# Three latent tiles projected for layer 1 inside layer 0's experts stage

## What is computed

```python
for l in range(2):
    last = l == 1
    h, hc = modulate(x, norm1_g[l], mod[0], mod[1]), modulate(xc, norm1_g[l], mod_c[0], mod_c[1])
    y, yc = token_mix(h, hc, ..., w_in[l], ..., not last)      # starts with h @ w_in: 1024 x 3104
    x = x + mod[2] * (y @ w_out[l])
    h2 = modulate(x, norm2_g[l], mod[3], mod[4])
    x = x + mod[5] * peer_ffn(h2, peer_wq[l], peer_subkeys[l], peer_u[l], peer_v[l])
    # layer 0 does the last three lines for the context xc too
return rms_norm(x, final_g)

def modulate(x, g, shift, scale): return rms_norm(x, g) * (1 + scale) + shift
def peer_ffn(h, ...):              # per token: 8 heads choose 16 experts each, 128 in all
    act = gelu(einsum('td,thkd->thk', h, u[eid]))             # u[eid]: one row of 4 KB per expert
    return einsum('thk,thkd->td', gate * act, v[eid])
```

## Time and profile before

| | us |
|---|---|
| median of 3 runs (lowest, highest) | 5386.06 (5382.54, 5390.33) |
| the profiled execution | 5427.65 |
| its span, first to last instruction | 5425.9 |
| granted TensorE clock over the span, mean | 0.705 |
| layer 0's last step (gelu start to gelu start) | 2581 to 2950 |
| the V rows that remain after it | 2950 to 3163 |
| layer 1's projection stage | 3168 to 3424 |

### The profile page before, as it was taken

How to read it: one execution, slowest core, us unless ns; L and a number is a source line. 1 busy time by engine, 2 the same in 40 slices (tenths; PEclk the granted TensorE clock), 3 DMA queues, 4 the chain that set the end, 5 groups by cost and what they waited for, 6 DMA issues and landing times. The chain is left out here.

```text
span 5425.9 us, 35743 instructions
## 1 busy us (share of the span) xinstructions
PE 2597.9 (48%) x11633; PEld 1150.5 (21%) x11633; DVE 2785.2 (51%) x6161; ACT 494.5 (9%) x1038; POOL 2963.2 (55%) x2672
## 2 busy tenths in 40 slices
PE   5977778323333333333333569668601233333344
PEld 2435555200010000000000134355400000000001
DVE  1138658976466465565443011664897646644410
ACT  1027520000000000000000000443000000000000
POOL 1003103877777777777776620130287777777765
PEclk9988998656656656566666789789755565655567
DMA  5401024899999999999999941012389999999998
GB/s 189 149 24 18 2 92 161 298 375 379 369 369 375 375 372 376 372 369 368 374 380 362 365 151 62 8 19 84 104 296 361 365 363 361 360 361 365 366 364 321
DMA packets 452198, 1468.20 MB, mean 271 GB/s; under 512 B 59259, under 2 KB 97359, under 8 KB 448943
## 3 DMA queue, kind: packets, MB, share of 16 engines
q0 software_dynamic: 368640, 1342.34, 65.8%
q1 hardware_dynamic: 72360, 99.62, 5.7%
q10 hardware_dynamic: 11014, 23.95, 1.4%
HBM read 1459.62 MB, written 6.13 MB: 270 GB/s over the span
## 5 line engine op out<-in xcount | busy, mean ns | idle before, releaser
L1812 DVE CUSTOM_DVE_ANT_0 experts_U<-experts_U,Y 128x1024 f32<-128x1024 f32 x1280 | 1566.8, 1224 | 1353.4 <-DMA experts_U<-in_peer_u_dram,experts_expert 1270.2
L1458 POOL DMA_INDIRECT experts_U<-in_peer_u_dram,experts_expert x1280 | 1383.3, 1081 | 1005.2 <-DVE experts_expert L1315 611.4
L1697 PE MATMUL experts_acc<-experts_V,experts_lent 128*32 128x512 f32 x4544 | 983.4, 1002 | 1836.0 <-DMA experts_V<-in_peer_v_dram,experts_turned 1774.7
L1473 POOL DMA_INDIRECT experts_V<-in_peer_v_dram,experts_turned x1136 | 1274.6, 1122 | 505.5 <-issue 336.0
L1697 PEld LDWEIGHTS experts_acc<-experts_V,experts_lent 128*32 128x32 f32 x4544 | 191.4, 153 | 2558.2 <-issue 2557.5
L371 PE MATMUL proj_acc<-proj_w,HT 128*128 128x512 f32 (+2 forms) x1280 | 486.4, 540 | 2.9 <-DVE PR L426 2.9
L734 POOL MEMSET glascore_Q<- 128x4096 f32 x2 | 7.0, 3512 | 560.4 <-POOLq L101 560.4
L371 PEld LDWEIGHTS proj_acc<-proj_w,HT 128*128 128x128 f32 x1280 | 242.0, 191 | 244.6 <-issue 213.6
L426 DVE COPY PR<-proj_acc 128x512 f32<-128x512 f32 (+2 forms) x80 | 49.5, 622 | 404.6 <-PE proj_acc L371 404.6
L1793 DVE TENSOR_TENSOR experts_lent<-experts_acc,experts_G 128x1024 f32<-128x1024 f32 x10 | 12.2, 1222 | 414.4 <-PE experts_acc L1697 351.1
L1226 PE MATMUL experts_keys<-experts_sub,experts_QT 64*128 64x128 f32 x320 | 41.5, 398 | 337.5 <-DVE experts_rest L1244 236.4
(11 more groups left out here) (259 smaller groups left out, 3165.3 us busy)
## 6 DMA issues: line engine op xcount, KB each, us to landing
experts_YT<-in_ada_w_dram SPq DMA_DIRECT2D x24, 1024.0 KB
proj_w<-in_w_in_dram SPq DMA_DIRECT2D x10, 2048.0 KB, 7.9
experts_U<-in_peer_u_dram,experts_expert POOLq DMA_INDIRECT x1280
experts_V<-in_peer_v_dram,experts_turned POOLq DMA_INDIRECT x1136
proj_ada<-in_ada_w_dram ACTq DMA_DIRECT2D x16, 1024.0 KB, 4.9
setup_ada<-in_ada_w_dram SPq DMA_DIRECT2D x8, 1024.0 KB, 17.5
experts_U<-in_w_out_dram SPq DMA_DIRECT2D x4, 2048.0 KB, 11.3
experts_V<-in_peer_wq_dram SPq DMA_DIRECT2D x4, 2048.0 KB, 21.4
```

What stands on the lines that cost most here:

```text
L1458: pool.indirect_dma_start(s.U[:, n % RING], None, u_rows, bass.IndirectOffsetOnAxis(ap=s.expert[:, j % 2, k:k + 1], axis=0)).then_inc(ug[n ...
L1473: pool.indirect_dma_start(into, None, v_rows, bass.IndirectOffsetOnAxis(ap=s.turned[:, i % 2, e:e + 1], axis=0)).then_inc(done, 16)
L1697: mm = nc.tensor.matmul(acc[32 * c:32 * c + 32, i % 2, half], s.spread[:, e * 32:e * 32 + 32], v_slot(V * GROUP + c)[0][:, 512 * half:512 ...
L1812: nc.vector.tensor_tensor_reduce(out=s.U[:, n % RING], in0=s.U[:, n % RING], in1=s.H[:, tiles[j]], scale=1.0, scalar=0.0, op0=ALU.mult, op ...
```

## The change

The constant `HIDDEN` = 3 is added: three latent tiles (3, 4, 5) of layer 1's projection are made in layer 0's experts stage.

- `experts` takes its tiles in the order 3, 4, 5, 2, 0, 1 in layer 0 (3, 4, 5, 2 in layer 1), so that the three are finished in `X` when the last step begins. `QT` is indexed by place in that order.
- In layer 0's last step SP broadcasts the three rows of layer 1's first norm, ACT squares the three tiles (into `half_out`) and loads w_in of layer 1 in 13 chunks of 240 columns (the last of 224) into two buffers in `QT`, VectorE scales and shifts, TensorE transposes through the search's PSUM banks `ps`, ACT copies into `Y`. From group 12 of the step on, TensorE does two products of 240 columns behind each group of V: 39 in all. ACT copies each out and stores it to the DRAM tensor `kept`.
- `project` in layer 1 norms and projects tiles 0, 1 and 2 only (17 products in place of 38), with the same seven chunks of weights. ACT loads the three kept tiles from DRAM into `PR` behind its part of the norm and waits for them before the stage ends.

The core of the diff, with the helper functions cut (their bodies are told above):

```diff
+HIDDEN = 3
 def project(nc, m, l, HT, PR, scratch):
+    t1 = NT - HIDDEN if last else NT
+    EARLY = min(t1 - 1, BANKS)
-        work = [(c, t) for c, (_, _, need) in enumerate(PROJ_CHUNKS) for t in range(NT) if need or not last or t >= CT]
+        work = [(c, t) for c in range(len(chunks)) for t in range(t1) if chunks[c][2] or not last or t >= CT]
             def _(act):
                 if not first:
+                    for t in range(t1, NT):
+                        act.dma_start(PR[:, t], m.pr[(t - t1) * P:(t - t1 + 1) * P]).then_inc(kept, 16)
+                    act.wait_ge(kept, 16 * HIDDEN)
                     return
 def experts(nc, m, l, t0, Y):
-    tiles = list(range(t0, NT))
+    tiles = list(range(NT - HIDDEN, NT)) + list(range(CT, NT - HIDDEN)) + list(range(t0, CT))
+        WIDTHS = [240] * 12 + [PROJ - 12 * 240]
+        units = [(c, i) for c in range(len(WIDTHS)) for i in range(HIDDEN)]
+        UNITS_AT = [(T - 1) * GROUPS + g for g in range(12, 32) for _ in range(2)][:len(units)]
+        TURN_AT = [(T - 1) * GROUPS + g for g in (8, 9, 11)]
+        MEAN_AT, SHIFT_AT, COEF_AT = [24, 30, 36], [27, 33, 39], 6
+                def load_chunk(c):
+                    act.dma_start(next_w[:, c % 2, :, 0:WIDTHS[c]], ...).then_inc(next_win[c % 2], 16)
+                def next_unit(u):
+                    c, i = units[u]
+                    act.wait_ge(next_prods, u + 1)
+                    if u >= 4:
+                        act.wait_ge(next_stored[u % 4], 16 * (u // 4))
...
+                    nc.scalar.activation(next_out[:, u % 4, 0:WIDTHS[c]], ps[:, u % 2, 0:WIDTHS[c]], ACT.Copy).then_inc(next_ev, 1)
+                    act.wait_ge(next_ev, u + 1)
+                    act.dma_start(m.pr[i * P:(i + 1) * P, 240 * c:240 * c + WIDTHS[c]], ...).then_inc(next_stored[u % 4], 16)
+                    if u == last_unit[c] and c + 2 < len(WIDTHS):
+                        load_chunk(c + 2)
+                def next_product(u):
+                    c, i = units[u]
+                    if i == 0:
+                        pe.wait_ge(next_win[c % 2], 16 * (c // 2 + 1))
+                    if u >= 2:
+                        pe.wait_ge(next_ev, u - 1)
+                    for k in range(KD):
+                        mm = nc.tensor.matmul(ps[:, u % 2, 0:WIDTHS[c]], next_HT[:, k, i * P:(i + 1) * P],
+                                              next_w[:, c % 2, k, 0:WIDTHS[c]], start=k == 0, stop=k == KD - 1)
+                    mm.then_inc(next_prods, 1)
```

More of the change, by code:

```diff
@@ L257, in norm_modulate @@
     ev0, ev1 = ht
-    tiles = list(range(t0, NT))
+    tiles = list(range(t0, t1))
     n = len(tiles)
-    streams = [0, 1] if t0 < CT else [1]
+    streams = [x for x in (0, 1) if any((t >= CT) == x for t in tiles)]
     @block.sync
@@ L377, in early @@
                     product(pe, i - 1)
-            norm_modulate(nc, m, l, m.a["norm1_g"][l], 0, 0, HT, st, block, ht, scratch, after=early, squares=not first)
+            norm_modulate(nc, m, l, m.a["norm1_g"][l], 0, 0, t1, HT, st, block, ht, scratch, after=early, squares=not first)
             @block.sync
             def _(sp):
-                for c, (c0, wd, _) in enumerate(PROJ_CHUNKS):
+                for c, (c0, wd, _) in enumerate(chunks):
                     if c >= WR:
@@ L1700, in _ @@
                         mm.then_inc(sums, 1)
+                    if more:
+                        for i in range(HIDDEN):
+                            if TURN_AT[i] == G:
+                                next_turn(i)
+                        for u in range(len(units)):
+                            if UNITS_AT[u] == G:
+                                next_product(u)
             @block.vector
```

120 lines of the change are left out of this document (106 added, 14 removed).

## The result

| kernel | runs | median us | range us |
|---|---|---|---|
| before | 4 | 5384.3 | 5381.8 to 5390.33 |
| changed | 4 | 5311.3 | 5305.31 to 5316.15 |

The ratio is 0.9862, 95% interval 0.9845 to 0.9879: the kernel is 73 us faster. The forecast was 5299.4 us, 87 us faster, in a range of 5270 to 5345. The direction and the range hold; the gain is 14 us less than forecast.

What follows compares the result with a forecast made beforehand. Layer 0's experts stage was taken as bound by its gathers (DMA), layer 1's projection by TensorE. Terms -121.5 + 32 + 1.3 + 1.5 = -86.7 us, from 5386.1 to 5299.4 us, range 5270 to 5345.

Steps and rivals of the forecast that it cites:

- The projection stage, -121.5 us: Layer 1's projection: 124.9 us of products and 3.1 of transposes leave TensorE, 6.5 us of waits for weights come.
- rival 4: Layer 1's projection: the kept tiles' 4.77 MB run into the weight loads and delay a chunk; 5317 us, chance 0.07.
- The clock and TensorE: Layer 0's last experts step: at clock 0.9 a group takes 9.3 of 11.5 us, products stay beside gathers; 0 us.
- Rival 2: Layer 0's last step: clock stays low and TensorE ends the groups, 102 us; 5369 us in all, chance 0.08.
- Weight chunks in time: Layer 0's last step: each chunk is needed 23 us after its load goes out; one landed in 12 us.
- rival 3: Layer 0's last step: weight loads starve behind gathers, TensorE waits, gathers run out of slots; 5454 us, chance 0.06.
- Rings and tables: Experts stage: ring stalls 0 (10 us in the range), gelu table reload 1.28 us, semaphores 1.5 us for both stages.
- The bytes, +32 us: Layer 0's last step: 19.05 MB added beside the gathers, priced between a lower end of 6 us and 51.
- the middle between 14 and 51: Price of the added bytes: 14 us at a 410 GB/s ceiling, 51 us at the full 374 GB/s byte price.
- Rival 1: Layer 0's last step: added bytes are absorbed like the adaLN loads, 6 us in place of 32; 5273 us, chance 0.12.
- the rule of the Trainium skill's page: DMAs issued from SP, ACT and GpSimd share the same 16 engines, so another queue brings no bandwidth: 51 us.

Runs made afterwards that it cites:

- few_matmuls: Changed kernel with one matmul in place of eight in each of the 39 moved products: 5095.0 us, against 5097.5 for the changed kernel.
- more_bytes: Changed kernel with nine more loads of 1 MB on SP's queue in the last step: 5134.7 us, against 5106.4 for the changed kernel.
- first set: Follow-up runs, on chip 12, of four partial versions of the change beside the kernel before, which took 5432.9 us there.
- third set: Follow-up runs on chip 0: kernel before 5158.6 us, changed kernel 5106.4, and two variants of the changed kernel with fewer or more bytes loaded.
- second and third set: Follow-up runs on chips 7 and 0: kernel before 5159.7 and 5158.6 us, unaltered changed kernel 5097.5 and 5106.4 us, beside variants of it.
- part2_alone: Changed kernel doing all moved work in layer 0's experts stage while layer 1's projection still makes all six tiles: 5470.5 us, against 5432.9 for the kernel before.

## Why the prediction came out as it did

- **The projection stage, -121.5 us:** right, and near in its terms. 121.5 us in the traces, 122.8 in the runs; TensorE's busy time in the stage falls by 125.8 us (238.0 to 112.2) for 128.0 forecast, the waits for weights are 4.74 and 0.99 us for 4.5 and 1.0. That the sum agrees to the tenth is luck. The kept tiles' 4.77 MB delayed nothing, so rival 4 falls.
- **The clock and TensorE:** right. 0.91 in the stretch of the products for the 0.9 taken, and in `few_matmuls` seven eighths of the moved products are worth 0 us in the step, 2.5 by the medians and 5 by the ratios. Rival 2 falls.
- **Weight chunks in time:** right. 2.3 us of waiting for them in the whole step; rival 3 falls for this kernel, though `more_bytes` shows that its chain exists.
- **Rings and tables:** the gelu's table 1.28 us as taken; the end of layer 0's experts stage 0.9 to 1.6 us for at most 1.4 (layer 1's was not read). VectorE's waits had more weight than I gave them: 14.3 us in place of some 10, with 3 us of gathers lost for 0.
- **The bytes, +32 us:** this is the term that was mis-sized, and the step that failed stands behind the sum: the profiled execution was 0.8% over the median, no stage looked disturbed, and so the difference was taken as it is. Some 25 us of the 0.8% lay in steps that the change doesn't touch, and the price of the bytes was another where these ran faster. The term was near right where I read it (31 us in the traces, 37.7 in the runs of the first set) and too small for the median runs of the result (48) and for faster ones (55 by the traces of the third set, 59 to 69 by the medians). The 32 itself was a choice, the middle between 14 and 51, so that it came within 1 us of the traces is luck. Its upper end was no bound either: the 51 us price a byte at 374 GB/s, while the added rows got 342 GB/s of engine time, 56 us for 19.05 MB. The mechanism, bytes that fill the slack first and are paid in full beyond it, fits both sets, but in the third the gathers got dearer too; that the slack was there in the runs was assumed.
- **Rival 1** (absorbed like the adaLN loads) falls everywhere: the step grew by 35 us and more. By the rule of the Trainium skill's page "DMA: Bandwidth & Descriptors", section "Issuing engines are not separate DMA queues", the prediction had 51 us; the runs of the result, with 48, and the second and third set's, with 59 and 69, stand nearer to it than my middle of 32 did; the first set's, with 38, don't.

## What to carry to other kernels

Work that is moved beside a DMA-bound stage costs the time of its bytes less what the stage left unused of the DMA engines, and this differs between sets of runs: `part2_alone` costs 38 us where the unchanged step moves 368 to 375 GB/s, and the changed kernel's step grew by 62 us where it moves 406. That is some 30 us of a change that gave 52 to 73. Before pricing added bytes, compare the profiled execution's time with the median; where they differ, don't count on the slack that the profile shows. Here the full byte price, 51 us, was nearer to the 48 of the runs than the 32 that counted on it. Bytes that serve several tiles should be loaded once for all of them: by the traces the first three tiles cost 31 to 55 us, the fourth 8. And bytes that an engine waits for in order cost more than their time when they come late: in `more_bytes` one late load of 1 MB held TensorE for 25.5 us and the gathers with it.

## What the runs showed of the hardware

- The same kernel's gathers of 4 KB rows ran at 368 to 375 GB/s (DMA share 0.98 to 0.99) in one set of runs and at 401 to 406 (1.02 to 1.03) in others, and the kernel took 5433 us in the one and 5159 in the others, 5% less. Each set ran on another chip; whether the chip or something else makes the difference was not tested.
- With all the added bytes beside the gathers, the step's total is 385 GB/s in the first set and 392 to 394 in the second and third. The rows of 960 bytes, loads and stores on ACT's queue, took 14% more engine time by the byte than the gathers in the traced execution of the result; whether the size of the row or the kind of queue does it was not tried.
- In the changed kernel three queues side by side didn't starve each other: the products waited 2.3 us in two times for their weights, while GpSimd's gathers kept the engines full. With four loads of 1 MB in a row on SP's queue (`more_bytes`), TensorE waited 25.5 us for the last one and the DMA share fell to 0.48 for 20 us.
